# Latents on the undivided input, weights asked for at once, one product for the bias lines and one repeated transfer, folded squares

## The reference

```python
n = _rms_norm(h, attn_norm)                    # h: 272 x 1024
proj = n @ w_in
c_q, c_kv, k_rope, dq, dk, dv = split(proj)    # c_q, c_kv: 256 wide each
q  = _rms_norm(c_q, q_norm) @ w_uq             # 8 heads of 96
kv = _rms_norm(c_kv, kv_norm) @ w_ukv
...
bias = bias_table[_t5_bucket(q_pos - k_pos)]   # 32 buckets x 4 heads
a = softmax(s1 * scale + bias) - lam * softmax(s2 * scale + bias)
...
# second block: cross attention on a memory of 256 tokens
k, v = split(rmsnorm(mem, norm_mem_g) @ wkv)
```

## Time and profile before

| | us |
|---|---|
| median of three runs | 1431.94 |
| the profiled execution, whole | 1431.57 |
| its span, first to last instruction | 1429.8 |
| PE matmul busy | 1393.1 (97%) |
| DVE / ACT / POOL busy | 974.9 / 680.1 / 703.8 |

### The profile page before, as it was taken

How to read it: one execution, slowest core, us unless ns; L and a number is a source line. 1 busy time by engine, 2 the same in 40 slices (tenths; PEclk the granted TensorE clock), 3 DMA queues, 4 the chain that set the end, 5 groups by cost and what they waited for, 6 DMA issues and landing times.

```text
span 1429.8 us, 28599 instructions
## 1 busy us (share of the span) xinstructions
PE 1393.1 (97%) x9910; PEld 1257.7 (88%) x9910; DVE 974.9 (68%) x1679; ACT 680.1 (48%) x1034; POOL 703.8 (49%) x348
## 2 busy tenths in 40 slices
PE   7999998999999999999999999999999989999997
PEld 6777688999999999988888888999999967899997
DVE  4524658889888888766666666544455854799987
ACT  4433554445455555543333333444455356655553
POOL 4313257778866666644444444444432545355441
PEclk9999999999999999999999999999999999999999
DMA  7421035667755555577777777665643423455552
GB/s 290 124 85 44 32 133 191 197 190 213 234 180 180 179 182 183 176 215 236 233 234 232 239 234 222 184 189 177 192 169 133 167 70 118 141 183 176 184 184 72
DMA packets 89994, 250.16 MB, mean 175 GB/s; under 512 B 10048, under 2 KB 35920, under 8 KB 89296
## 3 DMA queue, kind: packets, MB, share of 16 engines
q1 hardware_dynamic: 86112, 238.20, 53.0%
q10 hardware_dynamic: 3824, 11.17, 2.1%
HBM read 234.09 MB, written 15.24 MB: 174 GB/s over the span
## 4 chain that ended last, share of the span: by engine, by line
PE 90%; DVE 6%; ACT 2%; issue 1%; POOL 0%; ACTq 0%; DVEq 0%
PE ps L1788 47%; PE ps L2209 25%; PE ps L2196 4%; PE ps L2179 3%; PE ps L2017 1%; PE ps L1803 1%; DVE big L1156 1%; PE ps L2059 1%; PE ps L2037 1%; PE ps L1987 1%; DVE w_lo L1132 1%; DVE x_op L1165 1%; ACT w_hi L652 1%; PE ps L1877 1%; PE ps L1908 0%
## 5 line engine op out<-in xcount | busy, mean ns | idle before, releaser
L537 POOL TENSOR_TENSOR w_lo<-raw,w_hi 128x1024 fp32r<-128x1024 f32 x259 | 644.6, 2490 | 614.7 <-ACT w_hi L652 610.4
L1788 PE MATMUL ps<-x_op,w_hi 128*128 128x256 f32 (+1 forms) x3904 | 727.8, 287 | 8.3 <-POOL x_op L549 2.0
L1788 PEld LDWEIGHTS ps<-x_op,w_hi 128*128 128x128 f32 x3904 | 610.0, 192 | 22.4 <-issue 9.4
L1788 PE MATMUL ps<-x_op,w_lo 128*128 128x256 f32 (+1 forms) x1952 | 553.0, 283 | 0.0
L652 ACT ACTIVATE w_hi<-raw 128x1024 fp32r<-128x1024 f32 x400 | 420.2, 1054 | 262.9 <-PE ps L2209 206.7
L1788 PEld LDWEIGHTS ps<-x_op,w_lo 128*128 128x128 f32 x1952 | 373.7, 191 | 0.0
L2209 PE MATMUL ps<-w_hi,h_op 128*128 128x512 f32 x1008 | 280.7, 395 | 0.0
L1132 DVE TENSOR_TENSOR w_lo<-raw,w_hi 128x1024 fp32r<-128x1024 f32 x141 | 182.5, 1294 | 98.6 <-ACT w_hi L652 98.0
L2209 PEld LDWEIGHTS ps<-w_hi,h_op 128*128 128x128 f32 x1008 | 187.5, 188 | 43.3 <-issue 0.2
L2209 PE MATMUL ps<-w_lo,h_op 128*128 128x512 f32 x504 | 158.6, 395 | 0.0
L1506 DVE TENSOR_TENSOR work<-route_t,ps 128x1536 bf16<-128x1536 bf16 x64 | 112.3, 1754 | 8.7
(11 more groups left out here) (297 smaller groups left out, 1250.3 us busy)
## 6 DMA issues: line engine op xcount, KB each, us to landing
raw<-blocks SPq DMA_DIRECT2D x404, 512.0 KB, 3.6
early_store<-kv_mem SPq DMA_DIRECT2D x96, 128.0 KB, 1.7
work<-early_store SPq DMA_DIRECT2D x96, 128.0 KB, 3.8
big<-consts ACTq DMA_DIRECT2D x2, 1336.0 KB, 6.8
big<-h_t ACTq DMA_DIRECT2D x4, 272.0 KB, 4.1
big<-bias_lines ACTq DMA_DIRECT2D x8, 136.0 KB, 2.6
bias_lines<-route_t ACTq DMA_DIRECT2D x4, 264.0 KB, 2.6
res<-mem_t SPq DMA_DIRECT2D x1, 1024.0 KB, 10.1
```

Source lines behind the costliest of these rows:

```text
L537: pool.tensor_tensor(w_lo[:, s, :], raw[:, s, :], w_hi[:, s, :].bitcast(F32), ALU.subtract).then_inc(sem("lo_pool"), 1)
L1788: mm = pe.matmul(ps[:, m_bank, 0:T], w, xp, start=(k == 0 and j == 0), stop=(k == last and j == 2))
```

## The change

- `in_op`, a new tile over the later place of q and k, holds the gained but not normed input in two parts. ACT makes the upper halves straight from `h_t`, DVE the lower ones. The first four blocks use it (`undivided_in`); blocks 4 to 16 use the normed input as before. As the latents are normed themselves, the missing factor drops out, up to the 1e-6 in the root, which a third product with `eps_r2` adds to each latent sum.
- The weight loads no longer wait for `h_t`. The constants, `rel_bias`, `w_uq`, `w_ukv` and the bias windows move from ACT's queue to SP's; the memory input is loaded behind block 6. SP waits for the stored lines behind block 8.
- The four bias lines are one product with `rel_in` (32 x 4) as stationary operand, giving four rows. One transfer with a repeat over 128 stores them all.
- The squares of the input are made by POOL and ACT and folded by additions to two slices before the sum; those of the memory are folded on POOL, around its half of block 8. Both sums are two products instead of eight, and the sum for the input stands behind block 1, that for the memory behind block 5.
- The lower half of block 0 is DVE's.

```diff
         return None
+    if n == 0:
+        return "dve"
...
-            sp.wait_ge(sem("h_loaded2"), 16)
...
-            sp.dma_start(flat2(mem_t[:, :, :]), dram["mem_t"]).then_inc(sem("mem_loaded"), 16)
+            sp.dma_start(rel_in, dram["rel_bias"]).then_inc(sem("rel_loaded"), 16)
+            sp.dma_start(cst, dram["consts"][:, N_CONSTS_KEPT:]).then_inc(sem("cst_loaded"), 16)
+            sp.dma_start(kept[:, :], dram["consts"][:, 0:N_CONSTS_KEPT]).then_inc(sem("kept_loaded"), 16)
...
                 next_load(At(n))
+                if n == RING:
+                    sp.dma_start(flat2(w_uq), dram["w_uq"]).then_inc(sem("wu_loaded"), 16)
+                if n == RING + 1:
+                    sp.dma_start(flat2(w_ukv), dram["w_ukv"]).then_inc(sem("wu_loaded"), 16)
+                if n == RING + 2:
+                    sp.dma_start(flat2(mem_t[:, :, :]), dram["mem_t"]).then_inc(sem("mem_loaded"), 16)
+                if n == RING + 4:
+                    sp.wait_ge(sem("line_stored"), 16)
+                    for h in range(DH):
+                        for t in range(2):
...
+                            sp.dma_start(bias[:, h, t, :], src).then_inc(sem("bias_loaded"), 16)
...
+            for c in range(2):
+                at = slice(2 * c * NK, 2 * (c + 1) * NK)
+                pool.wait_ge(sem(f"h_loaded{c}"), 16)
+                pool.tensor_tensor(sq[:, at], flat2(h_t)[:, at], flat2(h_t)[:, at], ALU.mult).then_inc(sem("in_squares"), 1)
+            pool.wait_ge(sem("in_squares"), 2)
+            pool.tensor_tensor(sq[:, 0:2 * NK], sq[:, 0:2 * NK], sq[:, 2 * NK:4 * NK], ALU.add).then_inc(sem("in_squares"), 1)
...
+            los(B_IN, B_IN + 3)
+            norm_lo(R_ATTN, NK)
+            los(B_IN + 3, B_IN + 5)
+            pool.wait_ge(sem("block_used"), UNDIVIDED_IN)
             pool.memset(flat2(q_full), 0.0)
-            pool.memset(flat2(k_full), 0.0)
...
+            pool.memset(flat2(k_full), 0.0).then_inc(sem("heads_zero"), 1)
+            los(B_IN + 5, B_IN + 7)
+            pool.wait_ge(sem("rms_squares"), KT * (R_MEM + 1))
+            pool.tensor_tensor(sq[:, 0:4 * NQ], sq[:, 0:4 * NQ], sq[:, 4 * NQ:8 * NQ], ALU.add).then_inc(sem("mem_squares"), 1)
+            los(B_IN + 7, B_IN + 9)
+            pool.wait_ge(sem("mem_squares"), 1)
+            pool.tensor_tensor(sq[:, 0:2 * NQ], sq[:, 0:2 * NQ], sq[:, 2 * NQ:4 * NQ], ALU.add).then_inc(sem("mem_squares"), 1)
...
+                for k in range(2 * c, 2 * c + 2):
+                    act.activation(in_op[:, 0, k, :], h_t[:, k, :], ACT.Copy, scale=pcol("attn", k)).then_inc(sem("in_hi"), 1)
+                if c == 0:
+                    his(1)
             his(2)
...
+            for c in range(2, 4):
+                at = slice(2 * c * NK, 2 * (c + 1) * NK)
+                act.activation(sq[:, at], flat2(h_t)[:, at], ACT.Square).then_inc(sem("rms_squares"), KT // 2)
+
+            def lines_out():
+
+                act.wait_ge(sem("line_done"), 1)
+                act.activation(line[0:DH, 0:LINE // 2], ps[0:DH, 4, 0:LINE // 2], ACT.Copy)
+                act.activation(line[0:DH, LINE // 2:LINE], ps[0:DH, 5, 0:LINE - LINE // 2], ACT.Copy).then_inc(sem("line_ready"), 1)
+                act.wait_ge(sem("line_ready"), 1)
+                act.dma_start(scratch[:, 0:P], line[0:DH, :].unsqueeze(1).to_broadcast([DH, P, LINE])).then_inc(sem("line_stored"), 16)
...
+            evacuate_in(0)
+            root(R_ATTN, NK)
+            evacuate_in(1)
+            lat_squares(0)
+            act.wait_ge(sem("rms_root"), R_ATTN + 1)
+            act.activation(eps_r2, rt, ACT.Square, scale=math.sqrt(2 * EPS)).then_inc(sem("eps_r2"), 1)
+            norm_hi(R_ATTN, NK, 0, range(0, 2))
+            evacuate_in(2)
+            norm_hi(R_ATTN, NK, 0, range(2, 5))
+            lat_root(0)
+            norm_hi(R_ATTN, NK, 0, range(5, KT))
+            evacuate_in(3)
+            lat_squares(1)
+            lines_out()
+            evacuate_in(4)
+            lat_root(1)
...
             evacuate_in(5)
...
             act.wait_ge(sem("q_product"), 1)
             act.activation(flat2(q_mla), banks(4, 4)[0:QK, :], ACT.Copy, scale=pcol("qkq", rows=QK)).then_inc(sem("q_raw"), 1)
             act.activation(xf[0:QK, 0:HEADS * NQ], banks(4, 4)[0:QK, :], ACT.Square).then_inc(sem("q_squares"), 1)
             evacuate_in(6)
-            act.wait_ge(sem("line_stored"), 16 * DH)
...
+            act.wait_ge(sem("rms_sum"), R_MEM + 1)
+            act.activation(mem_rt, ps[:, 3, 0:NQ], ACT.Sqrt, scale=1.0 / D, bias=E_MODEL).then_inc(sem("rms_root"), 1)
             evacuate_in(7)
             v_out(0)
...
+                for k in range(2 * c, 2 * c + 2):
+                    dve.wait_ge(sem("in_hi"), k + 1)
+                    dve.scalar_tensor_tensor(out=in_op[:, 1, k, :], in0=h_t[:, k, :], scalar=pcol("attn", k),
+                                             in1=in_op[:, 0, k, :].bitcast(F32), op0=ALU.mult, op1=ALU.subtract).then_inc(sem("in_lo"), 1)
+                if c == 2:
+                    los(1)
+            los(2)
+            dve.wait_ge(sem("rms_squares"), KT)
+            step(dve.tensor_tensor(sq[:, 4 * NK:6 * NK], sq[:, 4 * NK:6 * NK], sq[:, 6 * NK:8 * NK], ALU.add))
+            dve.wait_ge(sem("in_squares"), 3)
+            dve.tensor_tensor(sq[:, 0:2 * NK], sq[:, 0:2 * NK], sq[:, 4 * NK:6 * NK], ALU.add).then_inc(sem("squares_folded"), 1)
+            inverse_root(R_ATTN, NK)
+            los(4)
+            norm(R_ATTN, h_t, "attn", NK, inverted=True)
...
+            def undivided_in(j):
+
+                n, m = At(B_IN + j), M_IN + j
+                if j == 0:
+                    pe.wait_ge(sem("hi_done"), 1)
+                else:
+                    arrived(n)
+                if bank_free(m) is not None:
+                    pe.wait_ge(*bank_free(m))
+                out, s = ps[:, m % 2, 0:NK], n.mod(RING)
+                for k in range(KT):
+                    if j == 0:
+                        pe.wait_ge(sem("in_lo"), k + 1)
+                    for part in range(2):
+                        pe.matmul(out, w_hi[:, s, k * P:k * P + P], in_op[:, part, k, :], start=(k == 0 and part == 0), stop=False)
+                if j == 0:
+                    arrived(n)
+                for k in range(KT):
+                    mm = pe.matmul(out, w_lo[:, s, k * P:k * P + P], in_op[:, 0, k, :], start=False, stop=(k == KT - 1))
+                mm.then_inc(sem("block_used"), 1)
...
                 for a, e, b in ((0, LINE // 2, 4), (LINE // 2, LINE, 5)):
-                    mm = pe.matmul(ps[:, b, 0:e - a], rel_rep[:, h, :], con("bucket", BUCKETS, cst)[:, a:e], start=True, stop=True)
+                    mm = pe.matmul(ps[0:DH, b, 0:e - a], rel_in, con("bucket", BUCKETS, cst)[:, a:e], start=True, stop=True)
                 mm.then_inc(sem("line_done"), 1)
...
+                pe.wait_ge(sem("eps_r2"), 1)
                 for k in range(2):
                     a = w * 2 * NQ + k * n
-                    mm = pe.matmul(ps[:, 2 + w, 0:n], ones[:, :], lat_sq[:, a:a + n], start=(k == 0), stop=(k == 1))
-                mm.then_inc(sem("lat_sum"), 1)
+                    pe.matmul(ps[:, 2 + w, 0:n], ones[:, :], lat_sq[:, a:a + n], start=(k == 0), stop=False)
+                pe.matmul(ps[:, 2 + w, 0:n], ones[:, :], eps_r2[:, NK - n:NK], start=False, stop=True).then_inc(sem("lat_sum"), 1)
...
+            undivided_in(0)
+            undivided_in(1)
+            pe.wait_ge(sem("squares_folded"), 1)
+            for k in range(2):
+                mm = pe.matmul(ps[:, 2, 0:NK], ones[:, :], sq[:, k * NK:(k + 1) * NK], start=(k == 0), stop=(k == 1))
+            mm.then_inc(sem("rms_sum"), 1)
+            undivided_in(2)
             latent_sum(0)
-            project_in(3)
-            relative_line(3)
+            undivided_in(3)
+            relative_lines()
             project_in(4)
...
             latent_sum(1)
...
+            pe.wait_ge(sem("line_ready"), 1)
+            pe.wait_ge(sem("heads_zero"), 1)
...
             project_in(5)
+            pe.wait_ge(sem("lat_root"), 2)
+            pe.wait_ge(sem("mem_squares"), 2)
+            for k in range(2):
+                mm = pe.matmul(ps[:, 3, 0:NQ], ones[:, :], sq[:, k * NQ:(k + 1) * NQ], start=(k == 0), stop=(k == 1))
+            mm.then_inc(sem("rms_sum"), 1)
             project_in(6)
+            pe.wait_ge(sem("rms_root"), R_MEM + 1)
             pe.wait_ge(sem("lat_ready"), 2)
             values(0)
```

More of the change, by code:

```diff
@@ L99 @@
 N_CONSTS_KEPT = 2 * 128
+Q_FULL = 21682
+UNDIVIDED_IN = 4
 def taken(n):
@@ L170, in build @@
                 pass
+        with nc.sbuf_tensor("before_q_full", [P, Q_FULL], F32):
+            with nc.sbuf_tensor("in_op", [P, 2, KT, NK], F32R) as in_op:
+                pass
         big = sb("big", [P, NKEYS * NQ])
@@ L234, in build @@
         mem_rt, mem_rb = acc_sb[:, 0:NQ], acc_sb[:, NQ:2 * NQ]
-        lat_sq = xf[:, 0:2 * NQ + 2 * NK]
```

(36 more changed lines are left out.)

61 lines of the change are left out of this document (6 added, 55 removed).

## The result

The changed kernel took 1452.03 us in the median of four runs (1451.73 to 1455.72), the one before 1431.95: ratio 1.0134, interval [1.0112, 1.0156]. The forecast was 1444.7 and its range ended at 1450.0: the direction and the places were right, and the time fell 2 us outside the range.

The account below looks back on a forecast made before the run. It took TensorE alone to bound the opening 80 us and everything behind. A 6.9 us early start, then stops before block 6 and the third values, left 13.1 late: 1431.6 + 13.1 = 1444.7, range 1436.5 to 1450.

Parts of the forecast that it names:

- The start: Opening to block 5's end: early products on the undivided input end block 5 at 49.6 against 56.5, 6.9 us early.
- Block 1 may start: Opening: operands and weight halves ready at 15.0 us, between 13.5 without DVE/POOL collision and 17.5 with three POOL operations.
- The folded sum: TensorE after block 1: block 1 takes 3.0, the sum four passes of 0.23, done at 19.0 us.
- Block 4 at 33.7: TensorE idles 6.2 us until POOL's lower half, so block 4 starts at 33.7 instead of 42.4.
- 13 × 0.11 = 1.4: Clock cost after each long TensorE stop: 23 products instead of 36 in 4 us, 1.4 us lost.
- The new wait at block 6: TensorE stops 9.1 us before the memory sum for POOL's second fold; first values at 65.3, 5.8 us late.
- The repeated transfer: Bias-line store from four partitions takes 40 us, holds back weight loads; third values at 85.5, 13.1 us late.
- from there to the third values: After the store lands: bias-load issues, block 9's landing, ACT's upper half, copy and `v_out(0)`, 10.8 us with gaps.
- the four deliver what one of the sixteen DMA engines moves, 28 GB/s: Rate taken for the bias-line store: 38 us plus 2, so 40 us.
- Rival 1: Bias-line store spread well enough to be free; only early gain and block 6 wait count, 5.8 late: 1437.4; chance 0.23.
- 34 by the forecast: Bias-line store: anything under 34 us is free, since TensorE comes for the third values only at 78.2.
- Rival 2: Fold ready when block 5 ends, saving 9.1, 1.4 and 1.2, and store spread: 5.9 us early, 1425.7; chance 0.04.

Follow-up runs that it names:

- Experiment 2: Changed kernel with SP's wait for the stored bias lines, and the bias loads, behind block 16 instead of block 8; slow store kept: 1441.59 us.
- experiment 5: Changed kernel with the bias lines stored from partitions 0, 4, 8 and 12 instead of 0 to 3, same bytes: 1447.5 us in one run.
- experiment 6: Changed kernel with the bias lines stored from all 128 partitions by four stores of 32 partitions each: 1441.09 us.
- experiment 3: Changed kernel with POOL's second fold ahead of its half of block 8 and SP's store wait eight blocks later: 1429.95 us.
- experiment 4: On experiment 3: POOL's half of block 4 before the normed input's lower halves, DVE's head-window copies behind the latent norms: 1429.83 us.
- experiment 1: Changed kernel with POOL's second fold of the memory squares ahead of its half of block 8: 1452.08 us.
- experiment 7: On experiment 3: 25 products of ones on TensorE in the idle stretch before block 4: 1434.1 us in one run.
- experiment 8: On experiment 4: memory sum before block 5, memory root on ACT before the copies of block 5 and q: 1424.69 us, ratio 0.9930.

## Why the prediction was wrong by 7 us

**The start came out right, partly by luck.** "Block 1 may start" at 15.0: 14.92. The forecast had DVE alone, 13.6, and put 1.4 on top for DVE slowed by POOL. DVE was not slowed: its eight operations and two lower halves took 7.3 us instead of 8.3. It waited, as the chain shows, for the last piece of `h_t`, which took 8.18 us to land beside the weights (3.5 to 4.7 in the kernel before) and which the forecast had called hidden. The first input product came at 7.60, not near 6 to 7. The folded sum 19.0: 19.27. Block 4 at 33.7 after 6.2 idle: 33.46 after 5.8. From there to the end of block 5 I had 15.9 and it was 17.3, since at the low clock block 4 alone took 5.6 instead of 3.1: the term "13 × 0.11 = 1.4" held the loss of one 4 us window, and here two were low.

**The new wait at block 6 was right.** 9.1 forecast, 9.1 measured, in the predicted order; the root 1.2 and 1.2. First values 66.9 instead of 65.3, the 1.6 coming from the clock before and after the stop. Experiment 2 gives this part by itself: 7.8 late instead of 5.8.

**The repeated transfer was the right mechanism with the wrong size,** and it is the step that failed: the store was put at 40 us and took 45.0. The forecast's chain against the measured one:

| | forecast | measured | difference |
|---|---|---|---|
| store issued | 33.3 | 32.45 | -0.85 |
| store lands | 40 later | 44.99 later | +5.0 |
| from there to the third values | 10.8 | 11.8 | +1.0 |
| clock | 1.4 | 2.4 | +1.0 |
| late behind block 9 | 13.1 | 19.3 | +6.2 |

The first term is the size of the store: "the four deliver what one of the sixteen DMA engines moves, 28 GB/s", plus 2. The rate was 24 over the whole time (1.08 MB in 45.0 us), and the reason was not right either: with the same busy share of the engines, rows from partitions 0, 4, 8 and 12 moved at 101 GB/s (experiment 5), so it was not the rate of one engine but what the four neighbouring partitions share. The second is the landing of block 9, 5.85 instead of 4.4, behind the eight bias loads, with 0.4 less in the rest of that chain. The third is the clock again. The rest of the 7.3 between 1444.7 and 1452.0, 1.1, is the median of the runs against a sum made from one execution, and I can't split it.

The Trainium skill has two rules here. "SBUF — State Buffer", "Door 1: The DMA port swizzle", puts partitions 0 to 3 behind one of sixteen ports, 27.6 GB/s for 1 MiB, and partitions 0, 4, 8 and 12 on four different ones: experiment 5 agrees in kind, 25 against 101 GB/s, and the measured 24 to 25 is 9 to 13% below the page. "DMA: Bandwidth & Descriptors", "Rules for kernel authors", confines a DMA to as many engines as its outermost dimension has: the busy share of 0.24 and 0.27, as much as four of sixteen, agrees, though no run changed that dimension alone. Both hold here at once; I had weighed them as alternatives.

**The rivals.** Rival 1, a free store at 1437.4, is what experiments 2, 5 and 6 made: 1441.6, 1447.5 (one run) and 1441.1. Its 5.8 was 2.0 short at the marker of experiment 2, by the clock, and the rest came behind the marker. Stores of 7.6 and 14.8 us cost nothing, as it said; where between 15 and 45 the price begins, 34 by the forecast, was not tried. Rival 2, 1425.7, was experiment 3: it came out at 1430.0. Its sum counted the root's 1.2 as saved with the fold, while the root stands in another queue behind q's copies and cost 2.5 and the clock.

**What stays open.** DVE's copies of eight rows took 7.20 us in the changed kernel, beside POOL's operand, half of a block and two fills, and 0.88 where experiment 4 has them. Which of the three holds it back was not tried. But they end at 37.28, 0.28 us behind the second fill,

```profile
35.10 1.90 POOL L625 MEMSET big<- 128x2176 f32 x1
```

and in the other six traces that have them there (experiments 1, 2, 3, 5, 6 and 7) it is 0.26 to 0.29, while POOL's next half runs on beside DVE: DVE seems to wait until the fills are through. The low clock 970 us behind the marker was not followed up.

## What to carry to other kernels

Before a wait is put into a queue that issues loads, name everything behind it: here one wait for a 45 us store, placed eight blocks earlier than it had to be, cost 11.5 us, and moving it gave all of that back. For a transfer that repeats a few partitions, ask first how many paths the source has, and spread the rows over the partitions (45.0 to 14.8 us) before counting bytes. And when a wait is removed, read on in every queue that the next consumer waits for: after the fold came the root on ACT, after block 4's half DVE's latent norm, and only the kernel that reordered all of them (experiment 8) was 0.7% faster than the one before.

## What was not expected of the hardware

- A repeated store to HBM from partitions 0 to 3 runs at 24 to 25 GB/s, from partitions 0, 4, 8 and 12 at 101 GB/s, with nearly the same busy share of the DMA engines, 0.24 and 0.27.
- DVE's two copies of 8 x 768 took 7.20 us beside POOL's work and 0.88 elsewhere, a factor of 8 for an operation that touches eight partitions.
- After stops of 5.8 to 9.2 us TensorE worked at the lower clock for 4 to 6 us: it cost 2.4 at block 4 (5.60 instead of 3.2), 1.8 at the memory sum and block 6 (5.80 instead of 4.0) and 2.4 at the third values and block 9, where one window of the kernel before had suggested 1.4.
